# Four stage borders of a one-core transformer step: output weights first, second norm by K-tile, early down tiles, token-major end

## What is computed

```python
h = rmsnorm(x, lp['n1']) * (1.0 + sc1) + sh1
... = split_columns(h @ lp['w_in'])
y = jnp.concatenate([y_a, y_b, y_c], axis=-1) @ lp['w_out']     # attention, conv, RWKV heads
x = x + g1 * y
h2 = rmsnorm(x, lp['n2']) * (1.0 + sc2) + sh2
u, gv = jnp.split(h2 @ w_up, 2, axis=-1)                        # 2048 -> 2 x 5632
u = depthwise_conv(u, dw_w, dw_b)                               # width 3 along tokens
x = x + g2 * ((jax.nn.silu(u) * gv) @ w_down)                   # 5632 -> 2048
y_prompt, y_sample = final rmsnorm(x)
```

## Time and profile before

| what | us |
|---|---|
| median of 3 runs | 2456.88 (2453.79 to 2462.15) |
| the profiled execution | 2458.6, of which its span is 2456.8 |
| PE busy in the span | 2213.2 (90%) |
| DVE busy | 1146.5 (47%) |
| ACT busy | 760.4 (31%) |
| mean granted clock of PE | 0.94 of full speed |

### The profile page before, as it was taken

How to read it: one execution, slowest core, us unless ns; L and a number is a source line. 1 busy time by engine, 2 the same in 40 slices (tenths; PEclk the granted TensorE clock), 3 DMA queues, 4 the chain that set the end, 5 groups by cost and what they waited for, 6 DMA issues and landing times.

```text
span 2456.8 us, 43926 instructions
## 1 busy us (share of the span) xinstructions
PE 2213.2 (90%) x19325; PEld 1957.1 (80%) x19325; DVE 1146.5 (47%) x2088; ACT 760.4 (31%) x1226; POOL 94.7 (4%) x140
## 2 busy tenths in 40 slices
PE   3789999999677888887987999999999999999996
PEld 2268888888555666667986999999999998887885
DVE  1222213554485778873336434444443443445444
ACT  2112222222353443432223333333332333333332
POOL 1000000000301111110000000000000000000000
PEclk8589999999876999998997999999999999999998
DMA  8977767776601000005323434334333344433341
GB/s 294 348 255 236 230 219 233 248 240 215 152 1 27 7 26 10 3 5 189 121 93 118 133 120 132 125 121 136 121 127 130 121 132 159 136 121 120 126 132 51
DMA packets 283038, 338.78 MB, mean 138 GB/s; under 512 B 9453, under 2 KB 268131, under 8 KB 280608
## 3 DMA queue, kind: packets, MB, share of 16 engines
q1 hardware_dynamic: 281008, 329.77, 41.9%
q0 software_dynamic: 1840, 6.20, 1.0%
HBM read 328.43 MB, written 10.28 MB: 138 GB/s over the span
## 4 chain that ended last, share of the span: by engine, by line
PE 79%; DVE 12%; DMA 5%; ACT 2%; issue 2%; POOL 0%; SPq 0%; DVEq 0%; POOLq 0%; ACTq 0%
PE ps L606 23%; PE ps L608 22%; PE ps L607 22%; DMA ring<-in_w_mod_dram 3%; PE ps L644 3%; PE ps L653 1%; PE ps L798 1%; PE ps L792 1%; PE ps L788 1%; DVE arena L1606 1%; DVE w_split L1311 1%; DVE u_buf L1687 1%; DMA arena<-in_x_sample_dram 1%; DVE stat L1467 1%; DMA ring<-in_w_out_dram 1%
## 5 line engine op out<-in xcount | busy, mean ns | idle before, releaser
L1311 DVE TENSOR_TENSOR w_split<-ring,w_split 128x1024 fp32r<-128x1024 f32 (+1 forms) x392 | 475.6, 1219 | 762.4 <-ACT w_split L1050 762.4
L1050 ACT ACTIVATE w_split<-ring 128x1024 fp32r<-128x1024 f32 (+1 forms) x392 | 406.6, 1050 | 729.3 <-PE ps L608 592.4
L606 PE MATMUL ps<-h_split,w_split 128*128 128x384 f32 x1776 | 599.6, 338 | 18.4 <-DVE w_split L1311 18.4
L608 PE MATMUL ps<-h_split,w_split 128*128 128x384 f32 x1776 | 596.5, 336 | 0.0
L607 PE MATMUL ps<-h_split,w_split 128*128 128x384 f32 x1776 | 596.4, 336 | 0.0
L606 PEld LDWEIGHTS ps<-h_split,w_split 128*128 128x128 f32 x1776 | 335.4, 189 | 30.0 <-issue 18.1
L607 PEld LDWEIGHTS ps<-h_split,w_split 128*128 128x128 f32 x1776 | 335.3, 189 | 0.0
L608 PEld LDWEIGHTS ps<-h_split,w_split 128*128 128x128 f32 x1776 | 335.2, 189 | 0.0
L606 PE MATMUL ps<-w_split,h_split 128*128 128x256 f32 x960 | 275.6, 287 | 9.3 <-DVE w_split L1311 9.3
L607 PE MATMUL ps<-w_split,h_split 128*128 128x256 f32 x960 | 272.6, 284 | 0.0
L608 PE MATMUL ps<-w_split,h_split 128*128 128x256 f32 x960 | 272.5, 284 | 0.0
(11 more groups left out here) (344 smaller groups left out, 2359.8 us busy)
## 6 DMA issues: line engine op xcount, KB each, us to landing
ring<-in_w_mod_dram SPq DMA_DIRECT2D x96, 1024.0 KB, 8.2
ring<-in_w_up_dram SPq DMA_DIRECT2D x88, 1024.0 KB, 5.1
ring<-in_w_in_dram SPq DMA_DIRECT2D x46, 1024.0 KB, 6.1
ring<-in_w_down_dram SPq DMA_DIRECT2D x44, 1024.0 KB, 5.4
ring<-in_w_out_dram SPq DMA_DIRECT2D x16, 1024.0 KB, 5.8
arena<-in_x_sample_dram SPq DMA_DIRECT2D x4, 1024.0 KB, 10.7
x_mid<-arena SPq DMA_DIRECT2D x1, 3072.0 KB, 10.2
h_f<-x_mid SPq DMA_DIRECT2D x1, 3072.0 KB, 12.8
```

Of the source, the lines that this page charges most:

```text
L606: mm(o_, lh, rh, start=start, stop=False)
L608: return mm(o_, ll, rh, start=False, stop=stop)
L1050: AC(wh[k % SPLITS][:, 0:width(n)], arrived(n), ACT.Copy).then_inc(s_hi, 1)
L1311: V.tensor_tensor(wl[k % SPLITS][:, 0:w], arrived(n), wh[k % SPLITS][:, 0:w].bitcast(F32), ALU.subtract).then_inc(s_lo, 1)
```

## The change

It touches four borders between stages; what is computed stays.

1. Ahead of the output projection SP issues the weight pieces of blocks 0 and 1 first and the x2 loads behind them. PE makes the gate rows of g1 behind block 0; ACT copies them ahead of the split of block 2's first part. DVE waits for x2 and the gate rows ahead of the first residual, as before.
2. The squares of the second norm are taken block by block (256 columns) while the projection runs, with a small sum at the end. The first four up parts are split before the norm. The normalised rows are written in four quarters of 512 columns; PE transposes a quarter (`turn2`) at a time: prompt blocks to banks 6 and 7, where ACT modulates them (`mod_p`), sample blocks in pairs to banks 4 and 5, where DVE modulates 256 columns at once (`mod_s`). Rounding and subtraction go by K-tile (384 columns). PE starts an up part when its own four K-tiles are ready, and transposes quarters 2 and 3 between parts.
3. Weight parts P_DOWN to P_DOWN + 3 and activation tile 0 are split before the last up tiles are written (tile 0 has a buffer of its own in the arena). PE starts down tile 0 without waiting for the last activations, and makes the gate rows of g2 behind tile 3; ACT copies them behind its tile 6. At half 1's first K-tile PE waits for two residual tiles at a time.
4. The last three K-tiles of half 1 are run token tile by token tile (`s_kt`). DVE does residual, root and scaling for one token tile, then the next; squares of the first half's columns are taken early (tile FT + 9), those of the last 1024 columns in two pieces. Each output row is scaled and stored in two halves.

```diff
@@ SP
             sp.wait_ge(s_fc, 3 * GROUPS)
-            for t, src in (...):
-                sp.dma_start(x2[:, t, :], src).then_inc(s_x2, 16)
             for j in range(D // BLK):
                 load_block(P_OUT + PARTS * j, a["w_out"][0], BLK * j, BLK)
+                if j == 1:
+                    for t, src in (...):
+                        sp.dma_start(x2[:, t, :], src).then_inc(s_x2, 16)
...
             for t in range(3):
-                sp.wait_ge(s_yf, t + 1)
-                sp.dma_start(dst, x3[:, t, :]).then_inc(s_out, 16)
+                for c in range(2):
+                    sp.wait_ge(s_yf, 2 * t + c + 1)
+                    sp.dma_start(dst[:, DOWN_W * c:DOWN_W * (c + 1)], x3[:, t, DOWN_W * c:DOWN_W * (c + 1)]).then_inc(s_out, 16)
@@ PE
-            gate_rows(2 * KT, s_gbp, s_gbc)
             for j in range(D // BLK):
...
+                if j == 0:
+                    gate_rows(2 * KT, s_gbp, s_gbc)
+            def turn2(q):
+                pe.wait_ge(s_xn2, q + 1)
+                if q >= 2:
+                    pe.wait_ge(s_hmp, 4 * (q - 1))
+                for k in range(4 * q, 4 * q + 4):
+                    last = tr(ps[:, 6 + q % 2, toks(k % 4)], xn2[:, 0, toks(k)], ident)
+                last.then_inc(s_xtp, 1)
+                for j in range(2):
+                    if q:
+                        pe.wait_ge(s_hms, 4 * (q - 1) + 2 * j + 2)
+                    for k in range(2):
+                        for t in range(2):
+                            last = tr(ps[:, 4 + j, P * (2 * k + t):P * (2 * k + t + 1)], xn2[:, 1 + t, toks(4 * q + 2 * j + k)], ident)
+                    last.then_inc(s_xts, 1)
             pe.wait_ge(s_oc, 3 * (D // BLK))
-            (12 groups of 4 transposes)
-            pe.wait_ge(s_h2, 12)
+            turn2(0)
+            turn2(1)
             for i in range(DFF // BLK):
...
+                        if i == 0 and w == 0:
+                            pe.wait_ge(s_h2, KQ * (p + 1))
...
+                        if i == 0 and w == 0 and p < 2:
+                            turn2(p + 2)
-            pe.wait_ge(s_uact, FT)
-            gate_rows(5 * KT, s_gb2p, s_gb2c)
-            pe.wait_ge(s_gb2c, 8)
+            pe.wait_ge(s_uact, FT - 2)
             for q in range(2):
-                for f in range(FT):
+                for f in range(FT - 3 * q):
                     i = q * FT + f
+                    pe.wait_ge(s_lo, rank(P_DOWN + i) + 1)
+                    pe.wait_ge(s_al, i + 1)
+                    for t in range(3):
+                        if i == 0 and t == 2:
+                            pe.wait_ge(s_uc, FT)
+                        if q == 1 and f == 0:
+                            if t == 0:
+                                pe.wait_ge(s_gb2c, 8)
+                            else:
+                                pe.wait_ge(s_dc, 2 * t)
+                        last = down_tile(q, f, t)
+                    last.then_inc(s_kd, 1)
+                    if i == 3:
+                        pe.wait_ge(s_uact, FT)
+                        gate_rows(5 * KT, s_gb2p, s_gb2c)
+            pe.wait_ge(s_lo, rank(P_DOWN + 2 * FT - 1) + 1)
+            pe.wait_ge(s_al, 2 * FT)
+            for t in range(3):
+                for f in range(FT - 3, FT):
+                    last = down_tile(1, f, t)
+                last.then_inc(s_kt, 1)
@@ ACT
+            def squares(j):
+                ac.wait_ge(s_oc, 3 * (j + 1))
+                for t in range(3):
+                    AC(xn2[:, t, ...], x2[:, t, BLK * j:BLK * j + BLK], ACT.Square, accum_out=ssq2[:, t, j:j + 1]).then_inc(s_ssq2, 1)
             for n in range(P_OUT, P_UP):
+                if n >= P_OUT + 3 * PARTS and n % PARTS == P_OUT % PARTS:
+                    squares((n - P_OUT) // PARTS - 3)
+                if n == P_OUT + 2 * PARTS:
+                    (the 8 copies of gate rows to gb)
                 hi(n)
+            for j in range(D // BLK - 3, D // BLK - 1):
+                squares(j)
+            for p in range(PARTS):
+                hi(P_UP + p)
+            squares(D // BLK - 1)
+            for k in range(KT + 1):
+                if k < KT:
+                    mod_p(k)
+                if k:
+                    h2_hi(k - 1)
...
+                    if i == DFF // BLK - 1:
+                        hi(P_DOWN)
+                        AC(ah[0], act[:, 0, :], ACT.Copy).then_inc(s_ah, 1)
...
+                if i == 6:
+                    (the 8 copies of gate rows to gb2)
+                if i == FT + 9:
+                    ac.wait_ge(s_al, FT + 6)
+                    ac.wait_ge(s_dc, 6)
+                    (3 squares of x3[:, t, 0:DOWN_W], accum_out=fsq[:, t, 0:1])
             for t in range(3):
-                ac.wait_ge(s_dc, 6 + 2 * t + 2)
-                AC(junk2, x3[:, t, :], ACT.Square, accum_out=stat[:, 32 + t:33 + t]).then_inc(s_fss, 1)
+                for c in range(2):
+                    ac.wait_ge(s_dc, 6 + 2 * t + c + 1)
+                    AC(junk2[:, cs], x3[:, t, cs], ACT.Square, accum_out=fsq[:, t, 1 + c:2 + c]).then_inc(s_fss, 1)
@@ DVE
+            for p in range(PARTS - 1):
+                lo(P_UP + p)
             residual(D // BLK - 1)
+            lo(P_UP + PARTS - 1)
+            link(V.tensor_reduce(stat[:, 24:27], ssq2, AX.X, ALU.add))
             inv_root(...)
+            xn2_part(0)
+            xn2_part(1)
+            for k in range(KT + 2):
+                if k >= 2:
+                    h2_lo(k - 2)
+                    dv.wait_ge(s_h2, k - 1)
+                if k < KT:
+                    mod_s(k)
+                if k in (1, 3):
+                    xn2_part(2 + k // 2)
...
+                if b == 2 * (DFF // BLK):
+                    lo(P_DOWN)
+                    dv.wait_ge(s_ah, 1)
+                    V.tensor_tensor(al[0], act[:, 0, :], ah[0].bitcast(F32), ALU.subtract).then_inc(s_al, 1)
+                    for i in range(1, SPLITS - 1):
+                        lo(P_DOWN + i)
...
+            for t in range(3):
+                dv.wait_ge(s_kt, t + 1)
+                residual2(1, t)
+                final(t)
```

More of the change, by code:

```diff
@@ L217, in build @@
         NA = 52900 - C_END - 4 * P - 2 * KT - 192 - 2 * KT - 64 - 11 - RING * PIECE - 2 * SPLITS * PART - 2 * KT * TOK - 2400
+        with ExitStack() as early:
+            sb("ahead_of_a", FT * TOK, F32, early)
+            afirst = sb("a_first", 2 * TOK, F32R, early)
         arena = sb("arena", NA)
@@ L323, in build @@
         ytmp, o = carve(ubuf, 0, 2, BLK)
[L324 removed]
+        mtmp, o = carve(ubuf, o, 4, TOK)
+        ssq2, o = carve(ubuf, o, 3, D // BLK)
+        assert o <= 2400
         act, o = carve(arena, 0, FT, TOK)
@@ L1013, in _, with down_tile @@
                         last.then_inc(s_blk, 1)
-            pe.wait_ge(s_uact, FT)
-            gate_rows(5 * KT, s_gb2p, s_gb2c)
-            pe.wait_ge(s_gb2c, 8)
+                        if i == 0 and w == 0 and p < 2:
+                            turn2(p + 2)
+            def down_tile(q, f, t):
+                w_hi, w_lo = parts(P_DOWN + q * FT + f, 1)
+                z = (q * FT + f) % 3
+                for c in range(2):
+                    cs = slice(512 * c, 512 * c + 512)
+                    last = three(ps[:, (6 * q + 2 * t + c) % 8, :], ah[z][:, toks(t)], al[z][:, toks(t)],
+                                 w_hi[:, 0, cs], w_lo[:, 0, cs], start=(f == 0), stop=(f == FT - 1))
+                return last
@@ L1222, in _ @@
                     rwkv_step(u, *step)
-            for n in range(8):
-                ac.wait_ge(s_gbp, n + 1)
-                AC(gb[:, n // 4, 512 * (n % 4):512 * (n % 4) + 512], ps[:, 6 + n % 2, :], ACT.Copy).then_inc(s_gbc, 1)
+            def squares(j):
+                ac.wait_ge(s_oc, 3 * (j + 1))
+                for t in range(3):
+                    AC(xn2[:, t, BLK * j:BLK * j + BLK], x2[:, t, BLK * j:BLK * j + BLK], ACT.Square, accum_out=ssq2[:, t, j:j + 1]).then_inc(s_ssq2, 1)
@@ new lines, in _, with mod_p @@
+                if n == P_OUT + 2 * PARTS:
+                    for m in range(8):
+                        ac.wait_ge(s_gbp, m + 1)
+                        AC(gb[:, m // 4, 512 * (m % 4):512 * (m % 4) + 512], ps[:, 6 + m % 2, :], ACT.Copy).then_inc(s_gbc, 1)
+                hi(n)
+            for j in range(D // BLK - 3, D // BLK - 1):
[3 more added lines that the diff above has]
+            squares(D // BLK - 1)
+            def mod_p(k):
+                ac.wait_ge(s_xtp, k // 4 + 1)
+                if k >= 4:
+                    ac.wait_ge(s_h2, k - 3)
+                AC(mtmp[:, k % 4, 0:P], ps[:, 6 + k // 4 % 2, toks(k % 4)], ACT.Identity, scale=scol[:, k, 0:1],
+                   bias=modcol[:, 3 * KT + k, 0:1]).then_inc(s_hmp, 1)
@@ L1238, in _, with h2_hi @@
+            def h2_hi(k):
+                ac.wait_ge(s_hms, k + 1)
+                ac.wait_ge(s_hmp, k + 1)
+                AC(hh[:, k, :], mtmp[:, k % 4], ACT.Copy).then_inc(s_hh2, 1)
```

(14 more changed lines are left out.)

150 lines of the change are left out of this document (69 added, 81 removed).

## The result

The changed kernel takes 2430.0 us (median of 4 runs, 2429.3 to 2430.1) against 2458.1 (2453.8 to 2462.2) before: a ratio of 0.988, 95% interval 0.986 to 0.990. The forecast was 2427, range 2419 to 2439. Its profiled execution took 2430.1 us, of which the span is 2428.3; before it was 2458.6 and 2456.8. So 28.5 us of the 29.9 forecast are there, by the spans of the profiled executions; by the medians it is 28.1.

What follows compares the result with a forecast made beforehand. PE, busy 90% of the span, was taken as the bound, with time only in its stops and low clock. Terms -0.1 + 18.2 + 7.5 - 0.7 + 5.0 = 29.9 us took the 2456.88 median to 2427, range 2419 to 2439.

Steps and rivals of the forecast that it cites:

- Part 1: Output projection: weights load first, PE starts 7.8 us earlier, gate rows behind block 0 cost 7.6; gain -0.1 us (-2.5 to +1.5).
- Part 2: Second norm to fourth up part: shorter norm, PE starts up projection 23 us earlier; gain 18.2 us (+4.0 to +20.7).
- The low clock: First up part: PE at its lower clock level after standing adds 2.5 us to 4.16.
- The waits behind the transposes: Up projection: PE waits about 1 us, twice, behind 12 transposes, before up parts 1 and 2.
- Rival 1: Up parts 0 to 3: short waits between them keep the clock low; +14.2 us, 2441 us; chance 0.13.
- Rival 2: Gate rows mid-stage cost 10.1 us each or leave a cooled clock behind them; +5 to +9 us, 2434; chance 0.10.
- Rival 3: Second norm: K-tile relay through DVE, ACT, DVE runs in series; 2446 to 2462 us; chance 0.02 slower, 0.03 between.
- Part 3: Start of down projection: PE goes straight on, 15.1 us gained less 7.6 for gate rows; gain 7.5 us (+5 to +7.8).
- Middle border: Between down projection halves: waiting for two residual tiles at once puts three more 0.23 us matmuls behind; -0.7 us (-1.3 to 0).
- Part 4: End: token-by-token finish gains 3.8 us, half-row stores 1.2; gain 5.0 us (+3 to +6), including a new 1.25 us PE stall.
- The rhythm of DVE: End: residual, square, root and scaling take DVE 7.0 us a token tile, 21.0 us in all, more than PE's 4.08.
- The tail: After the last scaling: halving the last 1 MB store shortens 4.3 us to 3.1.

Runs made afterwards that it cites:

- the few gates: The kernel before with one gate matmul instead of four for each of eight groups ahead of the output projection; 2461.4 us against 2461.2, ratio 1.0003.

## Why the prediction was right, point by point

The forecast was 1.4 us too good on 28.5. The tiles of the down projection took 3.3 us that it did not hold, and the end 0.5; part 1, part 2 and the middle border gave 0.3, 0.6 and 1.0 more than it said, and the untouched stretch 0.4. The 0.6 and the 1.0 hang on when the clock fell and rose, which changes from one execution to the next (below), so that the sum came so close is in part luck. The gains of parts 1 to 4 are not: each is read from its own stretch.

**Part 1** (forecast -0.1, measured 0.2). PE's first output matmul came at 1131.95 for 1132.3, the transfer took 5.72 for 5.8, the gate rows 7.43 for 7.6. That they had cost nothing before was right to 0.1% of the kernel (about 2.5 us), and PE's start behind the few gates shows it closer, 17.1 us for 17.0. It is why a part that moves the first matmul by 8 us is worth nothing.

**Part 2** (18.2, measured 18.8). The step by step chain ended where it should: PE started 16.00 us after the end of its last output matmul, for 16.0, with the single steps off by up to 0.3; one K-tile took 1.04 to 1.05 for 1.03. The low clock was mis-sized: part 0 took 6.05 us instead of 6.66, since the stretch at the low level was shorter than before, and in the other runs that keep this code it took 5.7 to 6.4. The waits behind the transposes were there, 0.83 us each:

```profile
1301.43 0.60 PE L1003 MATMUL ps<-consts,arena 128*128 128x128 f32 x4
1301.86 1.04 PE L1010 MATMUL ps<-consts,arena 128*128 128x128 f32 x8
1303.73 0.41 PE L616 MATMUL ps<-h_split,w_split 128*128 128x384 f32 x1 [0.83 <-DVE h_split L1764]
```

**Rival 1** fell. PE came to part 0 at the low clock, and the windows over the two waits behind it (the second ends at 1310.27) stay at the upper level:

```profile
1295.38:1299.00 3.62, 3.62 (x11) 3.62 (x12) 2.92 (x6) 1.69 (x4) 0.00 (x0) 0.50 1.09 348
...
1301.50:1304.00 2.50, 1.67 (x15) 1.46 (x14) 1.39 (x3) 1.94 (x5) 0.00 (x0) 1.00 0.86 274
1304.00:1308.00 4.00, 4.00 (x25) 3.96 (x24) 2.65 (x6) 1.44 (x4) 0.00 (x0) 1.00 0.01 4
1308.00:1312.00 4.00, 3.17 (x23) 2.96 (x22) 2.81 (x6) 3.07 (x8) 0.00 (x0) 1.00 0.01 2
```

0.83 us of standing, twice, 6.5 us apart, did not lower the clock. The Trainium skill, TensorE: Matmul & The Clock Gate (A second HAM failure mode), warns of swings from small idle stretches between groups of matmuls; stretches of this size and distance don't show it here.

**Rival 2** fell too: the gate rows cost 7.43 and 7.32 us in the middle of full work, with the granted clock at 1.00 in both stretches:

```profile
1151.00:1158.40 7.40, 7.40 (x66) 7.30 (x66) 1.23 (x1) 5.13 (x8) 0.00 (x0) 1.00 0.88 280
...
2051.00:2058.30 7.30, 7.30 (x65) 7.30 (x64) 0.56 (x1) 4.70 (x8) 0.00 (x0) 1.00 0.14 54
```

**Rival 3** fell: at 1.05 us a K-tile the relay ran two deep.

**Part 3** (7.5, measured 7.50). There is no gap on PE where the down projection starts (its last up matmul and its first down one):

```profile
2034.04 0.34 PE L618 MATMUL ps<-h_split,w_split 128*128 128x384 f32 x1
2034.21 0.39 PE L616 MATMUL ps<-w_split,a_first 128*128 128x512 f32 x1
```

What the step overlooked is what the buffer of tile 0 does afterwards. "Tile 0 has a buffer of its own in the arena" was in the description of the change, and the forecast priced its first use and not the 29 later ones: -3.3 us, the one term that was missing. Nothing in the rows of the kernel before could price it, since all its activation buffers lie at the same place modulo 256; a bound of zero stood where none was known.

**Middle border** (-0.7, measured +0.33, gains). The step was right in its mechanism, three more matmuls behind the last wait. The comparison was wrong: before, the five matmuls from 2256.89 on stood in the low clock, 1 us, and I took this to stay. Here the low stretch lay in the slack. As other executions gave 15.8 to 16.7 us, the forecast should have been a range, from +0.4 to -2.0.

**Part 4** (5.0, measured 4.50). The rhythm of DVE was right to 0.02 us: 2404.07, 2411.07, 2418.08. The tail was 3.15 for 3.1. What is missing stands ahead of DVE's first residual: 5.81 us from the last activation copy to it, where 1.25 + 4.08 = 5.33 were forecast. The copy, the subtraction and the handovers took the 1.25 (1.27, from 2398.26 to 2399.53). PE's first token tile took 4.24 us from its first matmul to the next tile's, for 4.08, and DVE started 0.3 after it. Only six of its 18 matmuls read a_first, so the place of that buffer explains at most 0.04 us of this; the rest is open. By the fit in the Trainium skill, DMA: Bandwidth & Descriptors (Anatomy of one DMA), the forecast had 4.4 and 3.2 us for whole and half rows, an estimate; the page fitted it to DMAs issued from GpSimd, and these stores are issued from SP. The tails measured were 4.3 before and 3.15 after. From issue to landing the stores took 3.9 and 2.7, half a us less than the fit, so the trace agrees with its step of 1.2 us and not with its fixed part. The half rows were right in spite of the page's rule for large transfers: they are worth 1.1 us.

## What to carry to other kernels

Ask of an instruction group not how long it is but what stands beside it where it is and where it goes: 64 matmuls were free under a load and cost 7.4 us behind it; inside the shorter wait they moved the start by 2.8 us and gave 1.8 of it back, since the clock was up when the projection began. When an edit adds a buffer, price every later use of it, and look at where it starts in SBUF. A stop of PE costs by what comes after it: the same low clock was free where the next matmuls had slack and 2 us where they were the path.

## What the hardware showed that was not expected

A matmul whose stationary operand (128 columns, float32 rounded) starts at another place modulo 256 bytes than 192, with the moving operand at 192, takes 6 to 7 ns longer from start to start, 4.19 to 4.20 against 4.08 us for 18 of them. It holds for 0, 64 and 224, the three other places tried. The weights' place was never moved. The down projection has 1584 such matmuls (88 tiles), so the place of one buffer group is worth 10.6 us by this reckoning (9.4 measured on 78 tiles), 0.43% of the kernel, more than part 3 or part 4 of this change.
